# Last chunk of each second product by token halves, and the layer norm's statistics with it

## What is computed

```python
f = _swiglu(x * (1.0 + sc) + sh, w_ffn_in[l, 0], w_ffn_out[l, 0])
x = _layernorm(DEEPNORM_ALPHA * x + 0.5 * g * f, ln_g[l, 0], ln_b[l, 0])

def _layernorm(x, g, b):
    mu = jnp.mean(xf, axis=-1, keepdims=True)
    var = jnp.mean(jnp.square(xf - mu), axis=-1, keepdims=True)
    return ((xf - mu) * lax.rsqrt(var + LN_EPS) * g + b).astype(x.dtype)
```

## Time and profile before

| | |
|---|---|
| runs | 2302.52 us median of 3 (2301.69 to 2305.2) |
| the profiled execution | 2299.79 us, its span 2298.0 us |
| busy, share of the span | PE 97%, PEld 91%, POOL 38%, DVE 37%, ACT 31% |
| mean granted TensorE clock | 0.98 |
| chain that ended last | PE 78%, issue 9%, DVE 5%, SP's queue 3%, POOL 3% |

### The profile page before, as it was taken

One profiled execution on the slowest core, in us unless ns is written; L12 is line 12 of the kernel. 1 busy time (PEld: TensorE's weight loads), 2 busy tenths in 40 slices (PEclk: granted clock), 3 DMA queues, 4 the chain that ended last, 5 costly groups with the idle time before them and its releaser, 6 DMA issues.

```text
span 2298.0 us, 44358 instructions
## 1 busy us (share of the span) xinstructions
PE 2219.0 (97%) x18518; PEld 2098.0 (91%) x18518; DVE 842.9 (37%) x1052; ACT 706.5 (31%) x1008; POOL 881.7 (38%) x402
## 2 busy tenths in 40 slices
PE   6999999989999899999999999999999999999997
PEld 5999999879885399999999899999989989999997
DVE  1222213327768463222123422222344372222234
ACT  4222222252235325222222522222232234222222
POOL 2344433414420244444433444443444453444443
PEclk8999999989998999999999999999999999999999
DMA  9233376537746442333563233357623332333331
GB/s 320 85 91 91 91 227 198 181 90 223 206 138 205 153 154 67 91 91 91 176 198 113 63 92 91 92 176 223 202 81 92 119 112 83 91 91 91 98 89 63
DMA packets 456097, 300.59 MB, mean 131 GB/s; under 512 B 20446, under 2 KB 435006, under 8 KB 455862
## 3 DMA queue, kind: packets, MB, share of 16 engines
q1 hardware_dynamic: 455990, 299.05, 43.0%
HBM read 293.46 MB, written 5.55 MB: 130 GB/s over the span
## 4 chain that ended last, share of the span: by engine, by line
PE 78%; issue 9%; DVE 5%; SPq 3%; POOL 3%; DMA 1%; ACT 1%; POOLq 0%; DVEq 0%; ACTq 0%
PE ps L904 73%; POOL w_lo L832 2%; PE ps L929 2%; SPq L623 1%; SPq L618 1%; POOL x L540 1%; DVE sq L1929 1%; PE ps L963 1%; SPq L724 1%; DMA ada_first<-w_ada 1%; DMA raw<-w_out_even 1%; DVE x L1888 0%; DVE sq_sum L1934 0%; DVE h_lo L1895 0%; ACT sq L1468 0%
## 5 line engine op out<-in xcount | busy, mean ns | idle before, releaser
L832 POOL TENSOR_TENSOR w_lo<-raw,w_hi 128x1024 fp32r<-128x1024 f32 (+1 forms) x303 | 788.8, 2604 | 1222.4 <-ACT w_hi L1525 1204.6
L904 PE MATMUL ps<-h_hi,w_hi 128*128 128x260 f32 x3584 | 1016.1, 284 | 6.5 <-POOL w_lo L832 6.1
L904 PE MATMUL ps<-h_hi,w_lo 128*128 128x260 f32 x3584 | 1013.3, 283 | 0.0
L904 PE MATMUL ps<-h_lo,w_hi 128*128 128x260 f32 x3584 | 1009.6, 282 | 0.0
L1525 ACT ACTIVATE w_hi<-raw 128x1024 fp32r<-128x1024 f32 (+1 forms) x303 | 341.5, 1127 | 1202.1 <-PE ps L904 1105.0
L904 PEld LDWEIGHTS ps<-h_hi,w_hi 128*128 128x128 f32 x3584 | 675.1, 188 | 13.5 <-POOL w_lo L832 6.6
L904 PEld LDWEIGHTS ps<-h_lo,w_hi 128*128 128x128 f32 x3584 | 674.5, 188 | 0.2
L904 PEld LDWEIGHTS ps<-h_hi,w_lo 128*128 128x128 f32 x3584 | 674.6, 188 | 0.0
L904 PE MATMUL ps<-hid_hi,w_hi 128*128 128x260 f32 x1408 | 399.6, 284 | 0.0
L904 PE MATMUL ps<-hid_hi,w_lo 128*128 128x260 f32 x1408 | 398.0, 283 | 0.0
L904 PE MATMUL ps<-hid_lo,w_hi 128*128 128x260 f32 x1408 | 397.9, 283 | 0.0
(11 more groups left out here) (306 smaller groups left out, 1750.8 us busy)
## 6 DMA issues: line engine op xcount, KB each, us to landing
raw<-w_ffn_in SPq DMA_DIRECT2D x173, 512.0 KB, 3.7
ada_w<-w_ada SPq DMA_DIRECT2D x112, 512.0 KB, 6.6
raw<-w_ffn_out SPq DMA_DIRECT2D x64, 704.0 KB, 4.4
pages<-cache_k SPq DMA_DIRECT2D x64, 256.0 KB, 3.5
pages<-cache_v SPq DMA_DIRECT2D x64, 256.0 KB, 3.4
raw<-w_in_even SPq DMA_DIRECT2D x27, 512.0 KB, 5.4
raw<-w_in_odd SPq DMA_DIRECT2D x23, 512.0 KB, 3.6
ada_first<-w_ada SPq DMA_DIRECT2D x10, 1024.0 KB, 11.7
```

What stands on the lines that cost most here:

```text
L832: pool.tensor_tensor(w_lo[:, k, 0:kt, :], raw[:, k, 0:kt, :], w_hi[:, k, 0:kt, :].bitcast(F32), ALU.subtract).then_inc(chunk_cut, chunks)
L904: mm = pe.matmul(ps[:, 2 * q + half, 0:HT], w[:, k, t, :], v[:, kt0 + t, half, :], start=start and t == order[0] and step == 0, stop=stop ...
```

## The change

The last chunk of each second product is done for the first token half over all weight tiles, and then for the second half (`halves_product`; the same matmuls in another order, with a semaphore of its own after the first half). DVE takes the last tile's residual by halves (`last_half`). In the first half it goes into `tile_sum` and, squared, into `sq_sum`; in the second TensorE adds it up from x and sq as it did before. The norm's sums, the copies of the mean, the transposes and the centring of tile 0 are done by halves.

The distance mean - shift is no longer made before the transpose. The early mean, which still stands in banks 4 and 5 after tile 2's product, is transposed there and its columns kept (`early_columns`); in the norm the mean itself is transposed, and the columns are subtracted (18 columns, both in SBUF). The samples are centred by POOL, ahead of its tiles, instead of by DVE. `delta_sq` moves from bank 4 to bank 0. The core of the diff:

```diff
+DRAINS, ADDS, SUMS, SQUARES, SQ_ADDS, STEPS = 2 * KT + 2, KT + 1, KT, KT + 1, KT - 1, 13
...
-        delta_sq = ps[:, 4, 320:320 + 2 * HPAD // 32].unsqueeze(2)
+        delta_sq = ps[:, 0, 320:320 + 2 * HPAD // 32].unsqueeze(2)
...
-        def centre(eng, n, part):
-            eng.wait_ge(mean_ready, n + 1)
-            for t in range(*((0, CENTRE), (CENTRE, KT - 1 if n + 1 == last else CENTRE_FIRST))[part]):
-                centre_tile(eng, n, t, part)
-        def centre_tile(eng, n, t, part):
+        def centre(pool, n):
+            pool.wait_ge(mean_ready, 2 * n + 2)
+            if n + 1 < last:
+                pool.tensor_tensor(x[:, :, :, HP:HT], x[:, :, :, HP:HT], all_samples(mean), ALU.subtract
+                                   ).then_inc(centred[1], 1)
+            for t in range(CENTRE, KT - 1 if n + 1 == last else CENTRE_FIRST):
+                centre_tile(pool, n, t)
+        def centre_tile(eng, n, t):
             end = HT if n + 1 == last else HP
-            eng.tensor_tensor(x[:, t, :, 0:end], x[:, t, :, 0:end], (mean[:, :, 0:end] if part else pair(2)[:, :, 0:end]),
-                              ALU.subtract).then_inc(centred[part], 1)
+            eng.tensor_tensor(x[:, t, :, 0:end], x[:, t, :, 0:end], mean[:, :, 0:end], ALU.subtract).then_inc(centred[1], 1)
...
+            def halves_product(c, k, q, kt, hi, lo, kt0=0, start=True):
+                pe.wait_ge(chunk_cut, c + 1)
+                for half in range(2):
+                    for t in range(kt):
+                        for step, (w, v) in enumerate(((w_hi, hi), (w_hi, lo), (w_lo, hi))):
+                            mm = pe.matmul(ps[:, 2 * q + half, 0:HT], w[:, k, t, :], v[:, kt0 + t, half, :],
+                                           start=start and t == 0 and step == 0, stop=t == kt - 1 and step == 2)
+                    mm.then_inc(chunk_used if half else half_made, 1)
...
-                pe.wait_ge(summed, (KT - 1) * (n + 1))
-                for half in range(2):
-                    pe.matmul(ps[:, 4 + half, 0:HT], mean_w, tile_sum[:, half, :], start=True, stop=False)
-                pe.wait_ge(sq_added, (KT - 2) * (n + 1))
-                for half in range(2):
-                    pe.matmul(ps[:, half, 0:HT], mean_w, sq_sum[:, half, :], start=True, stop=False)
-                pe.wait_ge(samp_added, KT * (n + 1))
-                for half in range(2):
-                    mm = pe.matmul(ps[:, 4 + half, 0:HT], mean_w, x[:, KT - 1, half, :], start=False, stop=True)
-                mm.then_inc(mean_done, 1)
-                pe.wait_ge(squared, KT * (n + 1))
-                for half in range(2):
-                    mm = pe.matmul(ps[:, half, 0:HT], mean_w, sq[:, (KT - 1) % 2, half, :], start=False, stop=True)
-                mm.then_inc(var_done, 1)
+                pe.wait_ge(delta_steps, STEPS * n + 2)
+                pe.wait_ge(summed, SUMS * (n + 1))
+                pe.matmul(ps[:, 4, 0:HT], mean_w, tile_sum[:, 0, :], start=True, stop=True).then_inc(mean_done, 1)
+                pe.wait_ge(sq_added, SQ_ADDS * (n + 1))
+                pe.matmul(ps[:, 0, 0:HT], mean_w, sq_sum[:, 0, :], start=True, stop=True).then_inc(var_done, 1)
+                pe.matmul(ps[:, 5, 0:HT], mean_w, tile_sum[:, 1, :], start=True, stop=False)
+                pe.matmul(ps[:, 1, 0:HT], mean_w, sq_sum[:, 1, :], start=True, stop=False)
+                pe.wait_ge(samp_added, ADDS * (n + 1))
+                pe.matmul(ps[:, 5, 0:HT], mean_w, x[:, KT - 1, 1, :], start=False, stop=True).then_inc(mean_done, 1)
+                pe.wait_ge(squared, SQUARES * (n + 1))
+                pe.matmul(ps[:, 1, 0:HT], mean_w, sq[:, (KT - 1) % 2, 1, :], start=False, stop=True).then_inc(var_done, 1)
...
+                    if t == KT - 1:
+                        for half in range(2):
+                            if half:
+                                act.wait_ge(mean_done, 2 * n + 1)
+                                act.activation(mean[:, 0], ps[:, 4, 0:HT], ACT.Identity).then_inc(mean_ready, 1)
+                            act.wait_ge(shifted, SQUARES * n + t + half + 1)
+                            act.activation(sq[:, t % 2, half], sq[:, t % 2, half], ACT.Square).then_inc(squared, 1)
+                        continue
+                    act.wait_ge(shifted, SQUARES * n + t + 1)
                     act.activation(sq[:, t % 2] if t else sq_sum[:, :, :], sq[:, t % 2], ACT.Square).then_inc(squared, 1)
             def norm_act(n):
-                act.wait_ge(mean_done, n + 1)
-                act.activation(mean[:, :, :], pair(2), ACT.Identity).then_inc(mean_ready, 1)
-                act.wait_ge(delta_steps, 8 * n + 3)
+                act.wait_ge(delta_steps, STEPS * n + 7)
                 act.activation(delta_sq, delta_col, ACT.Square).then_inc(delta_steps, 1)
-                act.wait_ge(delta_steps, 8 * n + 6)
+                act.activation(mean[:, 1], ps[:, 5, 0:HT], ACT.Identity).then_inc(mean_ready, 1)
+                act.wait_ge(delta_steps, STEPS * n + 10)
...
+            def last_half(n, half):
+                t, bank, a0 = KT - 1, 2 * ((KT - 1) % 2) + half, SQ_ADDS * n
+                xt, far = x[:, t, half, :], sq[:, t % 2, half]
+                g = mod[:, n % 3, t + 2 * KT, :]
+                samp = samp8[:, 4 * half:4 * half + 4]
+                dve.scalar_tensor_tensor(xt[:, 0:HP], ps[:, bank, 0:HP], g[:, 0:1], xt[:, 0:HP], ALU.mult, ALU.add
+                                         ).then_inc(drained, 1)
+                dve.tensor_tensor(samp, ps[:, bank, HP:HT], g[:, 1 + 4 * half:5 + 4 * half], ALU.mult).then_inc(drained, 1)
+                dve.wait_ge(drained, DRAINS * n + 2 * (t + half) + 2)
+                dve.tensor_tensor(xt[:, HP:HT], xt[:, HP:HT], samp, ALU.add).then_inc(samp_added, 1)
+                dve.wait_ge(samp_added, ADDS * n + t + half + 1)
+                if half == 0:
+                    dve.wait_ge(sq_added, a0 + t - 2)
+                dve.tensor_tensor(far, xt, shift[:, half, :], ALU.subtract).then_inc(shifted, 1)
+                if half == 0:
+                    dve.wait_ge(summed, SUMS * n + t)
+                    dve.tensor_tensor(tile_sum[:, 0], tile_sum[:, 0], xt, ALU.add).then_inc(summed, 1)
+                    dve.wait_ge(squared, SQUARES * n + t + 1)
+                    dve.wait_ge(sq_added, a0 + t - 1)
+                    dve.tensor_tensor(sq_sum[:, 0], sq_sum[:, 0], far, ALU.add).then_inc(sq_added, 1)
+            def early_columns(n):
+                dve.memset(ps[:, 4:6, HT:HPAD], 0.0).then_inc(delta_steps, 1)
+                dve.wait_ge(delta_steps, STEPS * n + 1)
+                dve.transpose(early_t[:, :].rearrange("p (h c) -> p h c", h=2), ps[:, 4:6, 0:HPAD]).then_inc(delta_steps, 1)
+                dve.wait_ge(delta_steps, STEPS * n + 2)
+                dve.tensor_copy(early_col, early_t_col).then_inc(delta_steps, 1)
...
+                        early_columns(n)
+                        dve.wait_ge(delta_steps, STEPS * n + 3)
...
+                dve.wait_ge(half_made, n + 1)
+                last_half(n, 0)
+                product_done((KT - 1) // 2, (KT - 1) % 2)
+                last_half(n, 1)
...
-                d0 = 8 * n + 1
-                dve.wait_ge(mean_ready, n + 1)
-                dve.memset(delta_at[:, :, HT:HPAD], 0.0).then_inc(delta_steps, 1)
-                dve.tensor_tensor(delta_at[:, :, 0:HT], pair(2), shift[:, :, :], ALU.subtract).then_inc(delta_steps, 1)
-                dve.wait_ge(delta_steps, d0 + 1)
-                dve.wait_ge(var_done, n + 1)
-                dve.transpose(delta_t[:, :], delta_at[:, :, :].rearrange("p h c -> p (h c)")).then_inc(delta_steps, 1)
-                dve.wait_ge(delta_steps, d0 + 2)
-                dve.transpose(var_t[:, :].rearrange("p (h c) -> p h c", h=2), ps[:, 0:2, 0:HPAD]).then_inc(delta_steps, 1)
-                dve.wait_ge(delta_steps, d0 + 4)
+                d0 = STEPS * n + 3
+                end = HT if n + 1 == last else HP
+                def centre_first(half):
+                    dve.tensor_tensor(x[:, 0, half, 0:end], x[:, 0, half, 0:end], ps[:, 4 + half, 0:end], ALU.subtract
+                                      ).then_inc(centred[0], 1)
+                dve.wait_ge(mean_ready, 2 * n + 1)
+                dve.transpose(delta_t[:, 0:HPAD], ps[:, 4, 0:HPAD]).then_inc(delta_steps, 1)
+                dve.wait_ge(var_done, 2 * n + 1)
+                dve.wait_ge(shifted, SQUARES * (n + 1))
+                dve.transpose(var_t[:, 0:HPAD], ps[:, 0, 0:HPAD]).then_inc(delta_steps, 1)
+                centre_first(0)
+                dve.wait_ge(mean_done, 2 * n + 2)
+                dve.transpose(delta_t[:, HPAD:2 * HPAD], ps[:, 5, 0:HPAD]).then_inc(delta_steps, 1)
+                dve.wait_ge(delta_steps, d0 + 3)
+                dve.scalar_tensor_tensor(delta_col, early_col, KT / EARLY, delta_col, ALU.mult, ALU.subtract
+                                         ).then_inc(delta_steps, 1)
```

(17 more changed lines are left out.)

67 lines of the change are left out of this document (36 added, 31 removed).

## The result

The changed kernel takes 2309.34 us in the median of 18 runs (2304.37 to 2311.54) and the kernel before 2301.9 us in as many (2297.18 to 2307.56). The medians lie 7.4 us apart; the ratio, by which this document goes, is 1.0028 with an interval of 1.0020 to 1.0035, which makes the change 6.4 us slower (4.6 to 8.1). The profiled execution lasts 2311.54 us with a span of 2309.0, which is 11.0 us more than the span before. Of the runs behind the ratios further down, one of e2 took 10524 us and is left out.

The account below looks back on a forecast made before the run. TensorE was taken as busy nearly always except in gaps after second products, where POOL ends close behind DVE. Feed-forward 0.8, mixers 5.3 and the rest 0 sum to 6.1 us, added to the 2302.52 median: 2308.6, range 2300 to 2312.

Parts of the forecast that it names:

- Feed-forward norms: Norms 0, 2 and 3: POOL's sample operation 0.26 us later each, 0.8 together; DVE's 2.5 us gain ends in waiting.
- Mixer norms: Norms 1 and 4: POOL's sample operation 2.66 us later each, 5.3 together, from the halves' work and a blocked subtraction.
- the work by halves: Mixer norms: paying each fixed cost twice makes the second difference end 1.5 us later, delaying POOL's weight cut.
- Blocked, the subtraction ends near 859.0: Mixer norms: DVE's 18-column subtraction, both inputs in SBUF, waits for POOL's whole weight cut; sample operation 2.66 us later.
- unblocked gap: Mixer norms: without the subtraction being blocked, POOL goes on from its cut and its sample operation comes 1.85 us later.
- The rest: Early columns, last norm, matmul order and DMA outside the five gaps: 0 us in the sum.
- The last norm: After the last sub-layer: POOL's sixth tile 0.26 us later, done at 2285.67; no change, 0.3 us either way.
- The cover for the early columns: Early mean's zeroing, transpose and copy, 1.0 us, hidden by DVE's waits or POOL's cut; uncovered, 1.0 us per mixer.
- Faster: First rival: normalisation, not POOL, counts; each of five norms gains up to 2.5 us, time 2290; chance 0.12.
- No measurable change: Second rival: subtraction not blocked or halves cost less; 4.5 us slower, time 2307.0, within 0.2%; chance 0.28.
- The third rival: Next product after each gap: TensorE's clock rises later, 3 us more over three norms, time 2311.6; chance 0.08.

Follow-up runs that it names:

- e2: Kernel before, with POOL centring two tiles instead of four before its sample operations; ratio 0.9996 to the kernel before.
- e1: Changed kernel, with POOL centring two tiles instead of four before its sample operations; ratio 0.9992 to the kernel before.
- e5: Changed kernel, with the two mixers' last chunk, residual, distance, sums and mean copy in one piece again; ratio 1.0006 to the kernel before.
- e7: Changed kernel, with five filler products of TensorE in each mixer gap before the first half sum; ratio 1.0018 to the kernel before.
- e3: Changed kernel, with ACT's copy of the second half's mean put ahead of its 18-column square; ratio 1.0006 to the kernel before.
- e4: Changed kernel, with the centring of the sample columns back on DVE instead of POOL; ratio 1.0016 to the kernel before.
- e12: Changed kernel, with POOL centring three tiles instead of four before its sample operations; ratio 1.0001 to the kernel before.
- e6: Changed kernel, with five filler products in each mixer gap and the early columns kept in PSUM instead of SBUF; ratio 1.0020 to the kernel before.

## Why the prediction was right

The direction, the place and the size were right: 6.1 us was the sum, 6.4 is measured, and 6.65 is read from the gaps.

**Feed-forward norms, predicted 0.26 each.** Right in every step: POOL starts 3.57 after the product's end (predicted 3.61), the first normalisation comes at 5.08 (5.1), and DVE's gain becomes a wait of 3.80 for ACT, which waits for POOL. The term was over-sized: 0.14 to 0.19 were measured, since POOL's start, its sample centring (0.28 for 0.31) and its four tiles (4.94 for 4.95) each took a little less. e1 and e2 show the claim beneath it, that POOL was as close to the end as DVE.

**Mixer norms, predicted 2.66 each; measured 3.22 and 2.92.** The first part, 1.5 for the work by halves, is right in size (1.48), though fixed costs paid twice are only 0.57 of it; the rest is the first half's two additions, which stand in the prediction's working but not in the reason that it gives. e5 takes most of the loss away (5.3 us of 6.14). The step that failed is "Blocked, the subtraction ends near 859.0": in the changed kernel it was not blocked. DVE waited 1.54 us for TensorE's second mean, and the cut was over by then. The prediction had costed TensorE's half sums at 0.44 each and not looked at when they could begin, 2.66 us after the product's end, nor at the clock. By the prediction's own sum an unblocked gap was to be 1.85 longer; it was 3.22 and 2.92, because the wait for TensorE, which was not in the sum, stood in for the block. That the size came out was therefore luck in part. With TensorE in time (e7) the block appears, and the gaps are 2.45 and 2.46 longer than before, beside the predicted 2.66. Both are shown.

**The rest.** The last norm was costed at nothing and changed by 0.04 us. The cover for the early columns held as described: they were held beside a cut that had held the differences before. Their copy was costed at 0.2 us and took 1.33 to 1.97, but hidden.

**The rivals.** "Faster" is excluded, and e1 shows from where it would have begun: two centrings less. "No measurable change" rested on the subtraction not being blocked. That happened, and the time did not follow, since another wait came in its place. The third rival, 3 us lost by a later clock in the next product, is not seen: in the eight windows of 2 us from its first matmul on, TensorE lost 12.9 us in the five gaps of the kernel before (2 us times one less the granted clock, summed) and 11.5 us in those of the changed kernel. Between the fourteen profiled executions this figure varies from 10.5 to 16.2, so that a difference of 1.4 says nothing either way. What was new is another place where the clock fell, the mixers' sums.

## What to carry to other kernels

Before making one chain shorter, look for the chain that ends beside it: here POOL's chain ended only 0.26 us before DVE's, and 2.5 us gained on DVE became a wait, until POOL's order was changed too. Halving a piece paid only where its first half could start earlier; where the engine was still busy with the piece before, the halves only added work (1.48 us). And a small operation is costed by what runs beside it: an 18-column one took 0.19 or 1.05 us according to where one operand lay and when it came.

## What was not expected of the hardware

TensorE's clock after the same short wait is not always the same. Of ten mixer gaps with half sums and no fillers (the changed kernel, e1, e3, e4, e12), all with 2.63 to 2.67 us of idleness before the sums, the sums ran partly at 0.50 in eight; in two, norm 4 of e3 and of e12, they all stayed at 1.00. In those two the subtraction met the cut and took 1.05 and 1.03 us. So the two ways to lose time in this gap take turns, in gaps that run the same code up to there. What decides between them no run shows.

The 18-column copy of the early mean, SBUF to SBUF, took 1.33 to 1.97 us in all six sub-layers of the changed kernel; a subtraction of as many columns takes 0.20. It was held, though it has only one input: in all six it ended 0.03 or 0.04 us after a weight cut of POOL that was running when it began. In e6, where its result lies in PSUM, it takes 0.19 or 0.20 in all six, each beside such a cut. DVE and POOL in sub-layer 0, of the changed kernel and then of e6:

```profile
360.95 1.97 DVE L1976 COPY early_col<-early_t 128x18 f32<-128x18 f32 x1
```

```profile
359.50 3.39 POOL L839 TENSOR_TENSOR w_lo<-raw,w_hi 128x1408 fp32r<-128x1408 f32 x1 [8.87 <-ACT w_hi L1552]
```

```profile
359.92 0.20 DVE L1981 COPY ps<-early_t 128x18 f32<-128x18 f32 x1
```

```profile
358.46 3.39 POOL L840 TENSOR_TENSOR w_lo<-raw,w_hi 128x1408 fp32r<-128x1408 f32 x1 [8.87 <-ACT w_hi L1557]
```

In e6 the difference behind the copy is held in its place (2.26 us).
